# Casts and low parts of the second feed-forward in another order, and the fifth block's low part on GpSimd

## The reference

```python
h = rms_norm(x, norm_mlp[l])
x = x + jnp.square(jax.nn.relu(h @ w_up[l])) @ w_down[l]
...
return rms_norm(x, norm_final)
```

## Time and profile before

| | |
|---|---|
| median of three runs | 2825.46 us |
| the profiled execution, its own time | 2824.13 us |
| its span | 2822.4 us |
| TensorE busy, granted clock | 2713.2 us, 0.989 of full |
| VectorE busy | 1765.8 us |
| ScalarE busy | 1136.1 us |
| GpSimd busy | 1785.2 us |
| stage of the change | from about 2156 us to the end |

### The profile page before, as it was taken

How to read it: one execution, slowest core, us unless ns; L and a number is a source line. 1 busy time by engine, 2 the same in 40 slices (tenths; PEclk the granted TensorE clock), 3 DMA queues, 4 the chain that set the end, 5 groups by cost and what they waited for, 6 DMA issues and landing times. The chain is left out here.

```text
span 2822.4 us, 39258 instructions
## 1 busy us (share of the span) xinstructions
PE 2713.2 (96%) x13371; PEld 2235.3 (79%) x13371; DVE 1765.8 (63%) x2194; ACT 1136.1 (40%) x1700; POOL 1785.2 (63%) x1214
## 2 busy tenths in 40 slices
PE   8999998999999999799999999999999999999998
PEld 7888886888888887678778778778787777777776
DVE  5334435556555555666676666667634788888888
ACT  4312316433333333545355354454425434433443
POOL 3333335777777766865565565466436888988893
PEclk9999999999999999899999999999999999999999
DMA  3111111111121212211121112112421111121112
GB/s 123 46 38 37 45 38 31 37 53 45 54 57 46 65 45 75 82 49 53 42 63 47 49 46 63 43 52 61 162 95 30 45 52 52 45 59 52 52 45 97
DMA packets 196117, 160.28 MB, mean 57 GB/s; under 512 B 5719, under 2 KB 176300, under 8 KB 196013
## 3 DMA queue, kind: packets, MB, share of 16 engines
q1 hardware_dynamic: 196013, 158.83, 18.6%
HBM read 143.08 MB, written 15.73 MB: 56 GB/s over the span
## 5 line engine op out<-in xcount | busy, mean ns | idle before, releaser
L340 POOL TENSOR_TENSOR w_lo<-w_raw,w_hi 128x512 fp32r<-128x512 f32 x351 | 495.3, 1420 | 293.9 <-ACT w_hi L334 293.9
L334 ACT CAST w_hi<-w_raw 128x512 fp32r<-128x512 f32 x351 | 209.7, 617 | 388.8 <-DMA w_raw<-in_w_in 121.2
L548 PE MATMUL PA<-h_hi,w_hi 128*128 128x512 f32 x636 | 261.5, 411 | 17.8 <-PEq L1037 5.4
L549 PE MATMUL PA<-h_lo,w_hi 128*128 128x512 f32 x636 | 250.2, 393 | 0.0
L550 PE MATMUL PA<-h_hi,w_lo 128*128 128x512 f32 x636 | 250.1, 393 | 0.0
L340 POOL TENSOR_TENSOR w_lo<-f_sums,w_hi 128x512 fp32r<-128x512 f32 x113 | 174.0, 1540 | 10.7 <-ACT w_hi L334 10.7
L340 POOL TENSOR_TENSOR w_lo<-hy_ring_sums,w_hi 128x512 fp32r<-128x512 f32 x96 | 139.1, 1449 | 61.7 <-ACT w_hi L334 61.7
L548 PE MATMUL PB<-f_t_hi,w_hi 128*128 128x512 f32 x424 | 168.7, 398 | 8.8 <-ACT hy_tm L2826 5.0
L396 POOL TENSOR_TENSOR w_raw<-w_raw,params 128x1024 f32<-128x1024 f32 x72 | 142.8, 2003 | 47.6 <-DMA w_raw<-in_ffn_w_up 46.6
L550 PE MATMUL PB<-f_t_hi,w_lo 128*128 128x512 f32 x424 | 165.8, 391 | 0.0
L549 PE MATMUL PB<-f_t_lo,w_hi 128*128 128x512 f32 x424 | 165.7, 391 | 0.0
(11 more groups left out here) (664 smaller groups left out, 8317.1 us busy)
## 6 DMA issues: line engine op xcount, KB each, us to landing
w_raw<-in_w_in SPq DMA_DIRECT2D x64, 512.0 KB, 5.1
w_raw<-in_ffn_w_up SPq DMA_DIRECT2D x42, 512.0 KB, 4.8
w_raw<-in_w_down SPq DMA_DIRECT2D x32, 512.0 KB, 3.7
w_raw<-in_w_up SPq DMA_DIRECT2D x30, 512.0 KB, 4.0
w_raw<-in_gla_w_in SPq DMA_DIRECT2D x24, 512.0 KB, 3.7
w_lo_raw<-in_ffn_w_down SPq DMA_DIRECT2D x44, 256.0 KB, 2.6
X<-in_x SPq DMA_DIRECT2D x8, 512.0 KB, 8.5
w_raw<-in_gla_w_out SPq DMA_DIRECT2D x8, 512.0 KB, 3.6
```

What stands on the lines that cost most here:

```text
L334: act.copy(self.slot(i, p)[0], source).then_inc(self.hi_done, 1)
L340: pool.tensor_tensor(lo, source, hi.bitcast(F32), ALU.subtract).then_inc(self.split, 1)
L548: pe.matmul(bank, ah[:, k, :], bh[:, k, :], start=(k == 0 and not more), stop=False, skip_group_check=more)
L549: pe.matmul(bank, ah[:, k, :], bl[:, k, :], start=False, stop=False, skip_group_check=more)
```

## The change

Five things change in `square_ffn`:

- **ScalarE casts the blocks of P1, P2 and P4 between the up weights** (`fall`, behind the second, third and fourth weight cast) and no longer all three behind the sixth. The order among them is now P1, P2, P4. Ahead of the first loop pass they are cast together in `rise(1)`.
- **VectorE makes the low parts in the order P4, P1, P7, P2** with the sums between them: the two sums that P7 needs stand right behind P4's low part (`LOWS`, `first_blocks`).
- **P5's low part moves from VectorE to GpSimd**, behind P3's (`LATE`).
- **The two large subtractions in X** go ahead of VectorE's first `combine`, and into it behind the third add.
- The up weights of chunk 1 are cast one more ahead of the first ReLU.

```diff
@@ -1972,9 +1972,10 @@
         WD = W_down.rearrange("(k p) n -> p k n", p=P)
         chunks = D_FF // (2 * P)
         DOWNS = TurnRing.DOWN_PRODUCTS
-        MADE = ("P4", "P1", "P2", "P7", "P3", "P5", "P6")
-        LATE = ('P3',)
-        EARLY = tuple(x for x in MADE if x not in LATE)
+        MADE = ("P1", "P2", "P4", "P7", "P3", "P5", "P6")
+        LOWS = ("P4", "P1", "P7", "P2", "P3", "P5", "P6")
+        LATE = ('P3', 'P5')
+        EARLY = tuple(x for x in LOWS if x not in LATE)
         PLACE = {"P1": 0, "P4": 1, "P2": 2, "P7": 3, "P3": 0, "P5": 2, "P6": 3}
         with ExitStack() as ctx:
             base = c.free + 48 * UNIT
@@ -2193,7 +2194,8 @@
 
                 def rise(i):
 
-                    a_high(i, "P4", "P1", "P2")
+                    if isinstance(i, int) and i == 1:
+                        a_high(i, "P1", "P2", "P4")
                     high(i, 6)
                     a_high(i, "P7")
                     keep(i)
@@ -2206,22 +2208,28 @@
                     relu_second(i)
                     following(0)
                     relu_first(i)
-                    for n in range(1, 6):
-                        following(n)
+                    following(1)
+                    following("P1")
+                    following(2)
+                    following("P2")
+                    following(3)
+                    following("P4")
+                    following(4)
+                    following(5)
 
                 high(0, 1, 2, 3, 4, 5)
                 keep(0)
                 weigh_second()
                 high(0, 6)
-                high(1, 0, 1, 2, 3)
+                high(1, 0, 1, 2, 3, 4)
                 relu_second(0)
                 relu_first(0)
-                high(1, 4, 5)
+                high(1, 5)
                 rise(1)
                 with act.Fori(2, chunks) as i:
-                    fall(i - 1, lambda n: high(i, n))
+                    fall(i - 1, lambda n: a_high(i, n) if isinstance(n, str) else high(i, n))
                     rise(i)
-                fall(chunks - 1, lambda n: n < 4 and ring.last_row_high(act, chunks, n))
+                fall(chunks - 1, lambda n: not isinstance(n, str) and n < 4 and ring.last_row_high(act, chunks, n))
                 last_high(1)
                 last_high(0)
                 tail.scalar(act)
@@ -2240,7 +2248,7 @@
                     k = PLACE[x]
                     dve.tensor_tensor(alo[k], BLOCK[x], ahi[k].bitcast(F32), ALU.subtract).then_inc(s["a_lo"], 1)
 
-                def combine(i):
+                def combine(i, between=None):
                     X, Z, W, Y = up_banks(i)
                     dve.wait_ge(s["kept"], i + 1)
                     dve.wait_ge(ring.used, ring.done(i, 3))
@@ -2250,6 +2258,8 @@
                     dve.wait_ge(s["u5"], i + 1)
                     dve.tensor_tensor(u22, u22, Z, ALU.add).then_inc(s["u7"], 1)
                     dve.wait_ge(s["u7"], i + 1)
+                    if between:
+                        between()
                     dve.wait_ge(ring.used, ring.done(i, 5))
                     dve.tensor_tensor(W, u22, W, ALU.subtract).then_inc(s["c21"], 1)
                     dve.wait_ge(ring.used, ring.done(i, 6))
@@ -2257,13 +2267,14 @@
 
                 def first_blocks(i):
 
-                    for x in ("P4", "P1", "P2"):
-                        a_low(i, x)
+                    a_low(i, "P4")
                     dve.tensor_tensor(A22, A21, A22, ALU.add).then_inc(s["a_sum"], 1)
                     dve.tensor_tensor(A21, A11, A21, ALU.subtract).then_inc(s["a_sum"], 1)
+                    a_low(i, "P1")
+                    a_low(i, "P7")
                     dve.wait_ge(s["a_sum"], i * 4 - 3)
                     dve.tensor_tensor(A11, A22, A11, ALU.subtract).then_inc(s["a_sum"], 1)
-                    a_low(i, "P7")
+                    a_low(i, "P2")
                     dve.wait_ge(s["a_sum"], i * 4 - 1)
                     dve.tensor_tensor(A12, A12, A11, ALU.subtract).then_inc(s["a_sum"], 1)
 
@@ -2288,7 +2299,6 @@
                     combine(i)
                     take(i, "P1")
                     take(i, "P2")
-                    a_low(i, "P5")
                     take(i, "P7")
                     a_low(i, "P6")
                     take(i, "P3")
@@ -2298,9 +2308,9 @@
                         last_lows()
                     take(i, "P6")
 
-                combine(0)
+                dve.wait_ge(ring.split, ring.done(0, 3))
                 dve.tensor_tensor(X12, X12, X22, ALU.subtract)
-                dve.tensor_tensor(X21, X21, X22, ALU.subtract)
+                combine(0, lambda: dve.tensor_tensor(X21, X21, X22, ALU.subtract))
                 chunk(1)
                 with dve.Fori(2, chunks - 1) as i:
                     chunk(i)
```

## The result

The changed kernel takes 2828.54 us, the median of 15 runs (2824.14 to 2834.55), against 2823.7 us of the kernel before in the same session: ratio 1.0018, 95% interval 1.0011 to 1.0025. The forecast was 2815.5 us and its range ended at 2828. The profiled execution of after took 2833.39 us.

A forecast was written before the change was run, and what follows sets the result against it. The ring of GpSimd, ScalarE, VectorE and back was the bound: 40.36 - 1.9 + 0.65 + 0.82 = 39.93 us a period. With first pass and last low part, 2824.13 - 9.9 + 1.3 = 2815.5 us, range 2806 to 2828.

The forecast's parts named there:

- the last of the sum: TensorE at P4 of the up products, waiting for VectorE's second add: 1.8 us a period in hand to cover it.
- GpSimd's side: GpSimd's wait ahead of its first row low part, 1.77 us, falls under 0.4 us; periods of 39.93 us.
- The price of the fifth block: One more low part on GpSimd a period, less stretching of the third block's: net 0.82 us a period.
- the gain of the weave: Earlier cast of P4's block and fewer VectorE operations up to P7's low part: row low parts start 1.9 us earlier.
- the ring of VectorE and TensorE: Rival, chance 0.20: VectorE's eight operations and two adds close a loop with TensorE, 40.7 us a period, 2826 us, no change.
- The first pass: Ahead of the loop, the moved X subtractions let P4's weight low part come earlier: first kept copy 1.7 us earlier.
- The end: The stretch from the last P3 on stays as it is.
- Full exclusion: Rival, chance 0.03: VectorE and GpSimd operations exclude each other, 1.98 us a pair, 41.4 us a period, 2836 us.

The follow-up runs named there:

- The kernel with the adds early: The changed kernel with P2's low part and the last sum on VectorE behind the three adds of its combine instead of ahead: 2819.96 us, ratio 0.9985.
- The filled kernel: The changed kernel with four matmuls that lead nowhere on TensorE ahead of its wait at P4 of the up products: 2824.89 us, ratio 1.0004.
- the lower row of the table: The changed kernel with P5's low part back on VectorE: 2823.66 us; the same with P2's low part and last sum behind the adds: 2810.15 us.

## Why the prediction was wrong

**The step that failed** is the last of the sum: "TensorE has 39.93 - 38.1 = 1.8 us a period in hand for it". The prediction saw that VectorE would be late next and that all eight operations stand ahead of the second add, and set the delay against a surplus, without laying out when TensorE reaches P4. The trace has it: TensorE is there at 2483.07, and VectorE's eight operations from 2470.11 at 1.70 us each end at 2483.7, with two adds still to come. The second add ends 1.9 us after TensorE is ready, and TensorE waits 2.03 us where the prediction had it wait at no cost. The surplus was a little smaller, too, since TensorE needs 38.38 us in a full period and not 38.1. Moving two operations behind the adds brought the time from 2828.54 to 2819.96 us; one more ahead of them to 2860.45 us.

**What was right is GpSimd's side.** Counted from the weighing at 2457.86, VectorE starts its first low part at w + 12.25 (forecast w + 12.25), the low part of P7 ends at w + 20.7 (20.8), L510 starts at w + 20.5 (20.6) and the first row low part at w + 21.9 (22.3). The kernel with the adds early runs at (559.85 / 14 =) 39.99 us a period, where 39.93 was forecast. The price of the fifth block, 0.82 us a period, was 0.79 when it was moved alone. Yet this price means that the move of the fifth block was a loss by itself, in each of the three orders in which it was tried. The forecast let it ride on the gain of the weave.

**The rival that came true** is the ring of VectorE and TensorE, given 0.20. It was put at 40.7 us a period and 2826 us. With the clock at its upper level a period with the long stall takes 40.40 us, about 0.04 more than before: 0.3 less than put. What speaks against it in the prediction, that a stalled GpSimd would make the eight operations shorter, happens in some periods, and hundredths of a microsecond decide it:

```profile
2396.21 0.68 DVE L2276 TENSOR_TENSOR f_u<-f_u,f_u 128x512 f32<-128x512 f32 x1
2396.28 1.77 POOL L510 TENSOR_TENSOR f_sums<-w_raw 128x512 f32<-128x512 f32 x1 [0.54 <-DMA w_raw<-in_w_down]
...
2416.32 1.96 DVE L2249 TENSOR_TENSOR f_a_lo<-f_u,f_a_hi 128x512 fp32r<-128x512 f32 x1
...
2499.69 1.03 DVE L2249 TENSOR_TENSOR f_a_lo<-f_u,f_a_hi 128x512 fp32r<-128x512 f32 x1
```

Here VectorE's sum L2276 starts 0.07 us ahead of GpSimd's L510 and takes 0.68 us, L510 takes 1.77 us, and the stall at P4 is 0.94 us. In the stretch shown further up it starts 0.08 us behind L510 (2478.48 and 2478.40) and takes 1.78 us, L510 1.31 us, and the stall is 2.03 us. So it goes in all 28 periods of the two profiled runs of the changed kernel; VectorE is first in seven of 14 and in three of 14. The shorter stall gains little, as its period is still 40.24 us: GpSimd's weighing does not come earlier with it, and P6's low part on VectorE, which now runs beside it, takes 1.93 to 1.96 us (2416.32) instead of 1.02 or 1.03 us (2499.69). That the rival's 569.8 us for 14 periods lies near the measured 568.55 us is partly luck: it had the ring too long and no fall of the clock in it.

**The clock was not priced at all.** No row of before's loop shows a fall: its stalls of 1.28 us brought none. The two profiled runs of the changed kernel have three and five falls between the kept copies of chunks 1 and 15, at 1.6 us each 4.9 and 8 us. The filled kernel, with none, is 4.45 and 7.84 us shorter in the same stretch. This also explains the size: from 559.85 (adds early) the ring adds 4.25 us and the clock the rest. Without the falls, by the filled kernel, the change comes to within 0.2% of before.

**The first pass** was to bring 1.7 us. From the stage's first matmul to the first kept copy of the loop it was 36.09 us before and is 35.95 now, 0.14 us. In their new places the two subtractions in X each stretch another operation of GpSimd. VectorE's rows for them, in the timeline of after:

```profile
2166.02 2.29 DVE L2312 TENSOR_TENSOR X<-X 128x2048 f32<-128x2048 f32 x1 [8.06 <-POOL w_lo L340]
...
2174.68 3.37 DVE L2313 TENSOR_TENSOR X<-X 128x2048 f32<-128x2048 f32 x1
```

and GpSimd's:

```profile
2166.07 3.40 POOL L426 TENSOR_TENSOR f_sums<-f_sums,w_raw 128x512 f32<-128x512 f32 x1
...
2175.85 3.35 POOL L418 TENSOR_TENSOR f_second_raw<-f_second_raw,f_second_raw 128x512 f32<-128x512 f32 x1
...
2184.41 1.30 POOL L426 TENSOR_TENSOR f_sums<-f_sums,f_second_raw 128x512 f32<-128x512 f32 x1
```

The sum at 2184.41 did shrink to 1.30 us, from the 3.23 of the earlier trace rows, but two others ahead of it now take 3.4 us. The prediction looked only at the operation that was freed. Nor did it price that P4's block is now cast last of the three there: VectorE's first low part, P4's, starts 30.6 us behind the stage's first matmul, where it was 27.5 us.

**The end** was taken to stay. From the last kept copy to the end of the span it is 67.5 us where it was 62.8. It has a P4 stall of 2.08 us and a fall of the clock of its own. The kernels with the adds early have 64.1 to 64.3 us there (65.2 us with P2's low part twice), so they give back at least 1.3 us of what their kept copies gain. With P5 on VectorE this is because the last kept copy comes before TensorE needs it, while before TensorE waited 1.30 us for it. With P5 on GpSimd TensorE still waits 0.45 us for it, and loses more at later stalls (2.16 us where it was 1.26 us, and a fall of the clock).

**Full exclusion** did not come as the rival had it: the operations in a row beside GpSimd follow at 1.70 us, and P7's low part ends at w + 20.7, not at w + 22.15. In a single pair the trace comes nearer to it. Of L2276 and L510 the one that starts first takes about its lone duration and the other is stretched, and where they start within 0.1 us of one another both are done 1.82 to 1.87 us after the first start, not far under 1.98 us. The Trainium skill (SBUF — State Buffer, Who interferes with whom) says that a VectorE operation with two SBUF inputs contends with GpSimd's reads, and that one with at most one SBUF input, outside VectorE's two-port modes, does not. Its division agrees with this trace: the low parts and sums take 1.70 us beside GpSimd, the adds L2255 and L2257, with one input in PSUM, 0.67 and 0.69 us.

**What stays open:** why a stall of the same 2.0 us is followed by a fall in some periods and not in others, and how many falls an unprofiled run has; the mean clocks say only that the changed kernel's runs have more of the lower clock. The stages ahead of the change, which it does not touch, ended 2.9 us later in the profiled run of after than in that of before; over all 13 profiled runs the first matmul of the stage starts between 2152.1 and 2160.6 us, so this lies within what the runs differ by. The account of the lower row of the table, P5's low part behind or ahead of the weighing, is read from two traces, and no run tests it.

## What to carry to other kernels

When a wait is shortened, lay out the times at which every engine reaches its next meeting point, and put on a shared engine first what another engine waits for: two operations moved behind three short adds were worth 8.6 us here. Price each part of a bundle by itself: the weave with early adds gains 13.6 us, and the fifth block's move takes back 9.8 of it. A stall of TensorE in a ring can cost more than its length, where the clock falls behind it; where GpSimd set the period, with the fifth block alone moved, five falls of six cost 0.1 us at most. Where VectorE and GpSimd meet, look which of the two starts first: that decides which one is stretched.

## What the runs showed of the hardware that was not expected

TensorE's clock fell behind stalls in the middle of dense work. Over all 13 profiled runs (the changed kernel twice, every other kernel once), from the kept copy of chunk 2 to the end, the idle times of TensorE and how many of them were followed by the lower clock within 4 us:

| idle time ahead of a matmul | stalls | followed by a fall |
|---|---|---|
| 0.85 to 1.5 us | 99 | 0 |
| 1.6 to 1.85 us | 12 | 3 |
| 2.0 to 2.2 us | 28 | 16 |
| 2.4 to 3.75 us | 22 | 16 |

It is not the length alone: in the kernel with P2's low part twice two stalls of 3.7 us brought no fall, and in the one with the fifth block alone moved all seven of 2.7 us did. While the clock is at the lower level a matmul step takes 0.42 to 0.43 us instead of 0.2266, and a fall cost 1.62 us. Work that leads nowhere, put into the stalls, kept the clock up: with ten such matmuls a period no fall was left in the loop, and the kernel took 16.6 us less.

Where an operation of VectorE with both inputs in SBUF, the memory that both engines read, and one of GpSimd started within 0.3 us of one another, the later one was stretched. L2276 took 0.68 us ahead of L510 and 1.78 us behind it, L510 1.77 and 1.31 us; a low part took 0.69 us ahead of a weighing and 2.37 us behind its start.

A VectorE subtraction of 128x2048 stretched one GpSimd operation of 128x512 beside it from 1.30 to 3.35 and 3.40 us, and itself took 2.29 us in one place and 3.37 in another.
